# Attention scores as rounded parts and remainders, with the values' projection moved ahead of the queries' and keys'

## What is computed

```python
proj = jnp.einsum('bsd,dc->bsc', x, w_in[l])            # 2048 -> 6144 columns
q_a, k_a, v_a, q_b, k_b, v_b = jnp.split(proj, splits, axis=-1)
q_a, k_a = apply_rope(q_a...), apply_rope(k_a...)       # 8 heads, 2 maps of 64 each
s = jnp.einsum('bqhmd,bkhmd->bhmqk', qi, k) * scale     # per head: two maps
a = p[:, :, 0] - lam * p[:, :, 1]                       # softmax of map 0 less lam times map 1
q_b, k_b = apply_rope(q_b...), apply_rope(k_b...)       # 8 heads, one map of 128
s = jnp.einsum('brhnqd,brhnkd->brhnqk', qb, kwin) * (D ** -0.5)
```

## Time and profile before

| | |
|---|---|
| median of 3 runs | 1095.04 us (1095.03 to 1095.20) |
| the profiled execution | 1094.98 us |
| its span, first to last instruction | 1093.2 us |
| PE busy | 1081.4 us, 99% of the span |
| DVE busy | 810.1 us, 74% |
| ACT busy | 568.4 us, 52% |
| granted TensorE clock, mean | 0.998 of full |
| TensorE score products (L559) | 96 records, from 76.0 to 324.9 us |

### The profile page before, as it was taken

One profiled execution on the slowest core, in us unless ns is written; L12 is line 12 of the kernel. 1 busy time (PEld: TensorE's weight loads), 2 busy tenths in 40 slices (PEclk: granted clock), 3 DMA queues, 4 the chain that ended last, 5 costly groups with the idle time before them and its releaser, 6 DMA issues.

```text
span 1093.2 us, 13845 instructions
## 1 busy us (share of the span) xinstructions
PE 1081.4 (99%) x5579; PEld 918.2 (84%) x5579; DVE 810.1 (74%) x893; ACT 568.4 (52%) x714; POOL 23.3 (2%) x45
## 2 busy tenths in 40 slices
PE   9999999999999999999999999999999999999996
PEld 8888888888888878888888888888888888888885
DVE  6587757666656685667699898666776678889998
ACT  6487757665544524445455454344454455554560
POOL 1000000010000000000000000000000000000001
PEclk9999999999999999999999999999999999999999
DMA  9857665557545834665656556466656655655852
GB/s 296 266 176 223 184 186 154 175 173 250 168 160 171 288 100 156 191 191 175 219 185 229 195 192 235 158 188 191 190 175 208 217 171 197 226 193 192 297 203 78
DMA packets 107903, 213.83 MB, mean 196 GB/s; under 512 B 6768, under 2 KB 37744, under 8 KB 107328
## 3 DMA queue, kind: packets, MB, share of 16 engines
q1 hardware_dynamic: 107216, 209.74, 59.4%
q0 software_dynamic: 624, 3.21, 1.0%
HBM read 210.83 MB, written 2.10 MB: 195 GB/s over the span
## 4 chain that ended last, share of the span: by engine, by line
PE 98%; DVE 1%; issue 0%; POOL 0%; ACT 0%; DVEq 0%
PE low_ps L780 11%; PE low_ps L619 10%; PE high_ps L780 10%; PE high_ps L800 8%; PE high_ps L798 8%; PE high_ps L799 8%; PE low_ps L512 6%; PE low_ps L516 6%; PE low_ps L514 6%; PE low_ps L785 5%; PE low_ps L624 5%; PE high_ps L785 5%; PE low_ps L800 2%; PE low_ps L798 2%; PE low_ps L799 2%; PE high_ps L559 1%
## 5 line engine op out<-in xcount | busy, mean ns | idle before, releaser
L1231 DVE TENSOR_TENSOR w_lo<-w_raw,w_hi 128x1024 fp32r<-128x1024 f32 x175 | 213.2, 1222 | 129.0 <-ACT w_hi L925 128.0
L925 ACT ACTIVATE w_hi<-w_raw 128x1024 fp32r<-128x1024 f32 x175 | 185.2, 1059 | 187.1 <-PE low_ps L516 66.9
L780 PE MATMUL low_ps<-x1T,w_hi 128*128 128x512 f32 x512 | 176.7, 393 | 0.0
L619 PE MATMUL low_ps<-xT,w_hi 128*128 128x512 f32 x448 | 156.8, 397 | 0.0
L780 PE MATMUL high_ps<-x1T,w_hi 128*128 128x512 f32 x448 | 155.0, 394 | 0.0
L785 PE MATMUL low_ps<-x1T,w_lo 128*128 128x256 f32 x512 | 136.9, 278 | 0.0
L1555 DVE TENSOR_TENSOR w_lo<-w_raw,w_hi 128x1024 fp32r<-128x1024 f32 x72 | 87.1, 1222 | 64.6 <-ACT w_hi L1124 64.6
L624 PE MATMUL low_ps<-xT,w_lo 128*128 128x256 f32 x448 | 122.3, 283 | 0.0
L1124 ACT ACTIVATE w_hi<-w_raw 128x1024 fp32r<-128x1024 f32 x72 | 76.1, 1059 | 88.8 <-PE low_ps L780 43.4
L785 PE MATMUL high_ps<-x1T,w_lo 128*128 128x256 f32 x448 | 119.8, 278 | 0.0
L798 PE MATMUL high_ps<-w_hi,hid 128*128 128x512 f32 x288 | 112.0, 389 | 0.0
(11 more groups left out here) (202 smaller groups left out, 1900.1 us busy)
## 6 DMA issues: line engine op xcount, KB each, us to landing
w_raw<-in_w_ff SPq DMA_DIRECT2D x208, 512.0 KB, 4.4
w_raw<-in_w_in SPq DMA_DIRECT2D x93, 512.0 KB, 4.1
more_raw<-in_w_ff SPq DMA_DIRECT2D x42, 512.0 KB, 5.3
w_raw<-in_w_out SPq DMA_DIRECT2D x32, 512.0 KB, 3.7
x_raw<-in_x_turned SPq DMA_DIRECT2D x8, 256.0 KB, 6.3
y<-in_x SPq DMA_DIRECT2D x8, 256.0 KB, 4.5
side_raw<-in_w_ff SPq DMA_DIRECT2D x4, 512.0 KB, 6.7
w_raw<-in_w_in SPq DMA_DIRECT2D x6, 256.0 KB, 5.2
```

The source lines that it names most:

```text
L619: return pe.matmul(banks[:, b, :], w_hi[:, slot, cols], xT[:, t, :, :].rearrange("p h t -> p (h t)"), start=(t == 0), stop=(t == KT - 1))
L780: return pe.matmul(banks[:, b, :], w_hi[:, slot, cols], x1T[:, t, :, :].rearrange("p h t -> p (h t)"), start=(t == 0), stop=(t == KT - 1))
L925: act.activation(w_hi[:, slot, :], w_raw[:, slot, :], ACT.Copy).then_inc(w_rounded, units)
L1231: dve.tensor_tensor(w_lo[:, slot, :], w_raw[:, slot, :], w_hi[:, slot, :].bitcast(F32), ALU.subtract).then_inc(w_split, units)
```

## The change

Scores become fp32r products of a high part and a remainder, for queries and keys alike.

- **Making the parts.** `rope` ends in `qk_rot` instead of `qT`/`kT`. Two steps after the chunk (`SPLIT_AFTER`), `round_qk` on ACT rounds it to the high part and `split_qk` on DVE subtracts for the remainder; for heads 0 to 7 both work in two instructions of 64 rows each, for heads 8 to 15 in one of 128. For the keys of heads 0 to 7, `double_k` on ACT writes the high part a second time onto the other 64 rows, one step later.
- **Heads 8 to 15.** Three full-height products for each query tile: hi·hi, hi·lo and lo·hi.
- **Heads 0 to 7.** For each map and query tile two products. The first, stacked, is 128 rows high: one half of the rows holds the query's high part, the other its remainder, and both meet the key's high part. The second is 64 rows high: the query's high part with the key's remainder (`k_low`), on rows 0 to 63 for map 0 and 64 to 127 for map 1.
- **One buffer.** `q_split`, `k_split`, `k_low` have one buffer for all groups; `rotate` and `copy_low` wait for other semaphores accordingly.
- **Order.** The values of groups 1 to 3 are projected before that group's queries and keys, no longer after. Head 0's scores come two units later, and so do head 1's.

The diff, cut to its core:

```diff
--- before.py
+++ after.py
 SCORE_AT = [24 * (h // 4) + 22 + (6 if h < HEADS - 4 else 3) * (h % 4) for h in range(HEADS)]
-SCORE_AT[0] += 2
+SCORE_AT[0] += 4
+SCORE_AT[1] += 2
...
-    IN_PLAN += [(2, group, 0)] + sorted(pairs) if group == 0 else pairs + [(2, group, 0)]
+    IN_PLAN += [(2, group, 0)] + (sorted(pairs) if group == 0 else pairs)
...
+SPLIT_AFTER = ROPE_AFTER
...
-    qT = at("qT", [P, 2, PER_GROUP, SEQ], F32, X0)
-    kT = at("kT", [P, 2, PER_GROUP, SEQ], F32, X0 + 8 * KB)
+    q_split = at("q_split", [P, PER_GROUP, 2, SEQ], F32R, X0)
+    k_split = at("k_split", [P, PER_GROUP, 2, SEQ], F32R, X0 + 8 * KB)
+    k_low = at("k_low", [P, PER_GROUP, SEQ], F32R, X0 + 28 * KB)
...
             pe.wait_ge(roped, 4 * g + 2 * (j // 2) + 2 if h > 1 else 3)
-            width = P // maps_of(h)
-            for m in range(maps_of(h)):
-                rows = slice(m * width, (m + 1) * width)
+            if maps_of(h) == 1:
                 for tt in range(TT):
-                    ins = pe.matmul(scores_ps[:, m, keys_of(tt)],
-                                    qT[rows, g % 2, j, tt * P:(tt + 1) * P],
-                                    kT[rows, g % 2, j, 0:(tt + 1) * P], start=True, stop=True)
+                    toks, keys = slice(tt * P, (tt + 1) * P), slice(0, (tt + 1) * P)
+                    pe.matmul(scores_ps[:, 0, keys_of(tt)], q_split[:, j, 0, toks],
+                              k_split[:, j, 0, keys], start=True, stop=False)
+                    pe.matmul(scores_ps[:, 0, keys_of(tt)], q_split[:, j, 0, toks],
+                              k_split[:, j, 1, keys], start=False, stop=False)
+                    ins = pe.matmul(scores_ps[:, 0, keys_of(tt)], q_split[:, j, 1, toks],
+                                    k_split[:, j, 0, keys], start=False, stop=True)
+                ins.then_inc(scores_done, 1)
+                return
+            pe.wait_ge(k_doubled, 2 * g + j // 2 + 1)
+            for m in range(2):
+                rows = rows_of(m)
+                for tt in range(TT):
+                    toks, keys = slice(tt * P, (tt + 1) * P), slice(0, (tt + 1) * P)
+                    pe.matmul(scores_ps[:, m, keys_of(tt)], q_split[:, j, m, toks],
+                              k_split[:, j, m, keys], start=True, stop=False)
+                    ins = pe.matmul(scores_ps[:, m, keys_of(tt)], q_split[rows, j, m, toks],
+                                    k_low[rows, j, keys], start=False, stop=True)
             ins.then_inc(scores_done, 1)
...
                 if n == 0:
+                    pe.wait_ge(qk_summed, 4 * GROUPS - 1)
+                elif n == 1:
                     pe.wait_ge(qk_summed, 4 * GROUPS)
-                elif n == 1:
-                    pe.wait_ge(v_copied, GROUPS)
...
             if r:
-                act.wait_ge(roped, r)
+                act.wait_ge(rope_terms, 2 * r)
             act.activation(qk_sum[:, :, :], in_banks(i)[:, :, SEQ:2 * SEQ], ACT.Copy).then_inc(
...
             act.wait_ge(qk_summed, r + 1)
+            if r:
+                act.wait_ge(roped, r)
...
+        def round_qk(r):
+
+            which, maps, heads = split_heads(r)
+            dst = (q_split, k_split)[which]
+            act.wait_ge(qk_turned, r + 1)
+            if maps == 1:
+                act.activation(dst[:, heads, 0, :], qk_rot[:, :, :], ACT.Copy).then_inc(qk_rounded, 1)
+                return
+            for m in range(2):
+                ins = act.activation(dst[rows_of(m), heads, m, :], qk_rot[rows_of(m), :, :], ACT.Copy)
+            ins.then_inc(qk_rounded, 1)
+
+        def double_k(r):
+
+            which, maps, heads = split_heads(r)
+            if which == 1 and maps == 2:
+                for m in range(2):
+                    ins = act.activation(k_split[rows_of(1 - m), heads, m, :], qk_rot[rows_of(m), :, :],
+                                         ACT.Copy)
+                ins.then_inc(k_doubled, 1)
...
+        def split_qk(r):
+
+            which, maps, heads = split_heads(r)
+            hi = (q_split, k_split)[which]
+            dve.wait_ge(qk_rounded, r + 1)
+            if maps == 1:
+                dve.tensor_tensor(hi[:, heads, 1, :], qk_rot[:, :, :], hi[:, heads, 0, :].bitcast(F32),
+                                  ALU.subtract).then_inc(roped, 1)
+                return
+            for m in range(2):
+                lo = (q_split[rows_of(1 - m), heads, m, :], k_low[rows_of(m), heads, :])[which]
+                ins = dve.tensor_tensor(lo, qk_rot[rows_of(m), :, :],
+                                        hi[rows_of(m), heads, m, :].bitcast(F32), ALU.subtract)
+            ins.then_inc(roped, 1)
```

More of the change, by code:

```diff
@@ L284, in hybrid_layer @@
     rope_terms, roped = sem("rope_terms"), sem("roped")
+    qk_turned, qk_rounded, k_doubled = sem("qk_turned"), sem("qk_rounded"), sem("k_doubled")
     low_copied, qk_summed, rotated = sem("low_copied"), sem("qk_summed"), sem("rotated")
@@ L355, in maps_of, with rows_of, split_heads @@
         return 2 if h < N_DIFF else 1
+    def rows_of(m):
+        return slice(m * HALF_DIM, (m + 1) * HALF_DIM)
+    def split_heads(r):
+        which, group, half = IN_PLAN[ROPE_CHUNK[r]]
+        return which, maps_of(PER_GROUP * group), slice(2 * half, 2 * half + 2)
     def in_chunk(i):
@@ L1015, in attention_after @@
         def attention_after(n):
+            if n - 2 in SPLIT_AFTER:
+                round_qk(SPLIT_AFTER.index(n - 2))
+            if n - 3 in SPLIT_AFTER:
+                double_k(SPLIT_AFTER.index(n - 3))
             if n in ROPE_AFTER:
@@ L1268, in rope @@
             dve.wait_ge(rope_terms, 2 * r + 2)
-            which, group, half = IN_PLAN[ROPE_CHUNK[r]]
-            dst = (qT, kT)[which][:, group % 2, 2 * half:2 * half + 2, :]
-            dve.tensor_tensor(dst, qk_cos[:, :, :], qk_rot[:, :, :], ALU.add).then_inc(roped, 1)
+            dve.tensor_tensor(qk_rot[:, :, :], qk_cos[:, :, :], qk_rot[:, :, :],
+                              ALU.add).then_inc(qk_turned, 1)
+        def split_qk(r):
[11 more added lines that the diff above has]
+            ins.then_inc(roped, 1)
         def mask_and_max(h):
@@ L1335, in attention_after @@
         def attention_after(n):
+            if n - 2 in SPLIT_AFTER:
+                split_qk(SPLIT_AFTER.index(n - 2))
             if n in ROPE_AFTER:
```

## The result

The changed kernel takes **1105.47 us** (median of 4 runs, 1105.33 to 1105.62) against 1095.03 for the kernel before, which ran beside it: 10.4 us slower, ratio 1.0094 with a 95% interval of 1.0082 to 1.0106. Forecast were 1104.6 us and a range of 1097 to 1113. The profiled execution took 1105.45 us, its span is 1103.7.

A forecast was written before the change was run, and what follows sets the result against it. The prediction took PE, busy 99% of the span, to bound the kernel. Its terms: 1094.98 + 9.4 (heads 0 to 7) + 0.2 (heads 8 to 15) = 1104.6 us, ACT and DVE 0; range 1097 to 1113.

The forecast's parts named there:

- PE's stream sets the time: Attention stage: PE runs product after product, so time moves with its stream unless a feeding engine causes a new wait.
- Heads 0 to 7, +9.4 us: Differential heads' scores: 8 changes of height a head against 2, so 48 more in all at 0.195 us each.
- The stream stays at 0.66: Scores of heads 0 to 7: eight single-pass products take 0.66 us a head without the height changes, as before.
- Heads 8 to 15, +0.2 us: Dilated heads' scores: six full-height fp32r products take 0.69 us against 0.66, +0.03 a head.
- ACT and DVE, 0 with no cover left: Rounding, remainders and key copies stay hidden, costing 0; weights' lead falls to 0.4 to 0.9 us at units 25 and 26.
- the free mix of heights: Rival at heads 0 to 7: 64-row products among full-height ones go at stream price, 1092.6 us; chance 0.15.
- half the price: Rival at heads 0 to 7: only pause or load is paid, 0.10 us a height change, 1098.5 us; chance 0.11.
- the slow narrow products: Rival at all heads' scores: 128-column fp32r products cost 0.22 us, as in float32, giving 1112.5 us; chance 0.11.

The follow-up runs named there:

- parts_made: Changed kernel with parts, doubled keys and new order kept, but scores as float32 products of the high parts alone, remainders left out; 1095.38 us.
- two_changes: Changed kernel with, for each of heads 0 to 7, all four stacked products first, then all four 64-row ones; 1096.45 us.
- full_height: Changed kernel with the 64-row products made 128 rows high, zeros on the half without the key's remainder; 1095.40 us.
- merged_narrow: Against full_height with float32 dilated heads and fourth chunk's parts four steps later: query tile 0's two narrow products made one wide, heads 0 to 7; 1092.62 us.

## Why the prediction was right

- **PE's stream sets the time**: held. PE's waits are the same 1.4 us, and parts_made, with all of the added work but the old products, is 0.3 us slower by the medians.
- **Heads 0 to 7, +9.4 us**: measured 8 x 1.22 = 9.8. The price of 0.195 us a change came from one subtraction (a differential head's 1.05 less the stream of 0.66, over two edges), and the parts it implied, 0.25 for a narrow product behind a change and 0.305 for a wide one, stand in the trace as 0.26 and 0.31. The runs with 8, 4, 2 and no changes a head (2.27, 1.38, 1.09, 0.92 us) carry it, and say more than the forecast did: what the alternation cost over a stream of the same products is 1.35 us of the 2.27. The price is an average and no constant: with two changes a head the scores took 0.07 us more than it gives. What inside TensorE makes the pause and holds the load back is not shown.
- **The stream stays at 0.66**: held in this sense only, that a product behind a change costs its bare columns. In a stream the same eight cost 0.92, since a narrow one is worth 0.11 there, not 0.055.
- **Heads 8 to 15, +0.2 us**: 0.3 by the starts, 0.5 to 0.7 by the run that takes it back, whose interval is wider than that. The 0.11 us for a narrow fp32r product, taken from the transposes, is what was measured (315.21 to 315.32); the 81 ns that the Trainium skill gives (TensorE: Matmul & The Clock Gate, Back-to-back issue gap) was not.
- **ACT and DVE, 0 with no cover left, 0.4 to 0.9 us at units 25 and 26**: measured 0.48 at unit 25 (split ended at 75.48, needed at 75.96) and 0.35 at unit 26, a little under the forecast. The stretch of 78 to 80 us that the forecast named for unit 25 is unit 26's. The one risk of that step showed only when PE became faster: at unit 30, where the lead was not worked out, two_changes and parts_made lost 0.4 us and full_height 0.6.
- **The rivals**: the free mix of heights, half the price and the slow narrow products are each refuted by the rows at head 1 or at the dilated head.
- **What is left**: 10.4 measured less 10.1 by the starts. The opening gave 0.1 of it (8.69 against 8.60 for the start of unit 1); the remaining 0.2 is inside the spread of the runs.

## What to carry to other kernels

Count the changes of height (rows in use) in a stream of products before counting passes: in the changed kernel each cost 0.15 to 0.19 us over a product's own slot, more than the product. Where a small product must stand among full-height ones, pad it with zeros to full height, or gather the small ones so that they share two edges and run side by side. And weigh narrow products by their loads: with a load before each, a product of 128 columns cost 0.11 us here and one of 256 only 0.12, so two of 128 columns with the same weights were better as one of 256.

## What the runs showed that I had not expected

- Padding with zeros, which doubles the rows of four products, makes a head cheaper (0.92 us) than the float32 products side by side (1.05). The kernel as a whole stayed only as fast as before until the queues of ACT and DVE ahead of unit 30 were relieved, and even then (1094.14) its interval just touches no gain; the first clear gain is merged_narrow's.
- In two_changes the 64-row products are issued as map 0 narrow, map 0 wide, map 1 narrow, map 1 wide, and yet their loads begin two at a time and all four fit into 0.43 us: products on different halves of the rows pair up across the order of the program.
- GpSimd's copies took 1.7 times as long as ScalarE's, and each of DVE's subtractions that began while one ran took 0.3 us longer, of 64 rows or of 128 (1.01 against 0.68, 1.52 against 1.22).
